# A two-block transformer on one core: small tables moved between the large tiles of SBUF

## The reference, cut to what matters

```python
# first block, layer l: 1024 x 2816 in, 1024 x 1024 out
hx = rmsnorm(x, g_pre) * (1 + scale) + shift
q, k, v, ga, uf, gf, zc, bc, cc, gc = split_cols(hx @ w_in, PROJ_SIZES)
x = x + gate * rmsnorm(gated_merge(a, ga, f, gf, s, gc, w_out), g_post)

# second block, layer l: two gated products around a mixer
x = x + 0.5 * m2 * swiglu(ada_norm(x, g0, m0, m1), ffn_w_in[l, 0], ffn_w_out[l, 0])
x = x + m5 * mixer(ada_norm(x, g1, m3, m4), ...)        # even: attention + mLSTM, odd: GLA
x = x + 0.5 * m8 * swiglu(ada_norm(x, g2, m6, m7), ffn_w_in[l, 1], ffn_w_out[l, 1])

def swiglu(h, w_in, w_out):
    a, b = jnp.split(h @ w_in, 2, axis=-1)              # 1024 -> 2 x 2816
    return (jax.nn.silu(a) * b) @ w_out                 # 2816 -> 1024
```

## Time and profile before

| | |
|---|---|
| runs | 2320.84, 2322.02, 2312.03 us, median 2320.84 |
| span of the profiled execution | 2314.2 us (6.6 us under the median; its own time outside the profiler isn't given) |
| instructions | 46991, of them 19320 matmuls and 19320 weight loads |
| busy | matmul 96%, weight load 90%, VectorE 49%, ScalarE 37%, GpSimd 8% |
| TensorE's granted clock | 0.987 of 2.4 GHz over the span |
| DMA | 312.5 MB read, 135 GB/s over the span |

### The profile page before, as it was taken

One profiled execution on the slowest core, in us unless ns is written; L12 is line 12 of the kernel. 1 busy time (PEld: TensorE's weight loads), 2 busy tenths in 40 slices (PEclk: granted clock), 3 DMA queues, 4 the chain that ended last, 5 costly groups with the idle time before them and its releaser, 6 DMA issues. The chain is left out here.

```text
span 2314.2 us, 46991 instructions
## 1 busy us (share of the span) xinstructions
PE 2227.1 (96%) x19320; PEld 2091.2 (90%) x19320; DVE 1145.4 (49%) x1930; ACT 846.8 (37%) x1384; POOL 176.3 (8%) x150
## 2 busy tenths in 40 slices
PE   6999999899999999998999999999999999999998
PEld 5986798799999999976999999999999998979998
DVE  5227375653433445456653333454343446487665
ACT  4226454632221233248432222243232234455444
POOL 0003112100000010501200000010000010001000
PEclk9999999999999999999999999999999999999999
DMA  9853544445676244520354666242233233225573
GB/s 297 234 167 86 172 133 104 128 147 154 186 216 186 86 131 117 149 80 28 102 175 141 190 207 189 84 126 85 81 114 94 86 96 101 74 82 146 168 202 112
DMA packets 515900, 315.76 MB, mean 136 GB/s; under 512 B 16035, under 2 KB 513274, under 8 KB 515622
## 3 DMA queue, kind: packets, MB, share of 16 engines
q1 hardware_dynamic: 515160, 313.45, 46.1%
q10 hardware_dynamic: 590, 0.16, 0.0%
HBM read 312.50 MB, written 1.06 MB: 135 GB/s over the span
## 5 line engine op out<-in xcount | busy, mean ns | idle before, releaser
L1118 PE MATMUL ps<-h_hi,w_hi 128*128 128x256 f32 x3376 | 728.0, 280 | 3.5 <-DVE h_lo L1726 1.7
L1118 PE MATMUL ps<-h_lo,w_hi 128*128 128x256 f32 x3376 | 720.6, 278 | 0.0
L1118 PE MATMUL ps<-h_hi,w_lo 128*128 128x256 f32 x3376 | 720.6, 278 | 0.0
L1118 PEld LDWEIGHTS ps<-h_hi,w_hi 128*128 128x128 f32 x3376 | 537.8, 189 | 22.9 <-issue 21.6
L1118 PEld LDWEIGHTS ps<-h_lo,w_hi 128*128 128x128 f32 x3376 | 539.4, 189 | 0.1
L1118 PEld LDWEIGHTS ps<-h_hi,w_lo 128*128 128x128 f32 x3376 | 537.9, 189 | 0.0
L1960 DVE TENSOR_TENSOR w_lo<-stage,w_hi 128x1024 fp32r<-128x1024 f32 x227 | 285.0, 1258 | 441.5 <-ACT w_hi L1467 440.9
L1467 ACT ACTIVATE w_hi<-stage 128x1024 fp32r<-128x1024 f32 x227 | 236.6, 1055 | 334.4 <-PE ps L1118 200.4
L1960 DVE TENSOR_TENSOR w_lo<-deep,w_hi 128x1024 fp32r<-128x1024 f32 x184 | 226.1, 1234 | 226.9 <-ACT w_hi L1467 225.2
L1467 ACT ACTIVATE w_hi<-deep 128x1024 fp32r<-128x1024 f32 x184 | 191.9, 1055 | 179.7 <-PE ps L1118 141.4
L1118 PE MATMUL ps<-g_hi,w_hi 128*128 128x256 f32 x1100 | 232.9, 280 | 0.2
(11 more groups left out here) (413 smaller groups left out, 2858.0 us busy)
## 6 DMA issues: line engine op xcount, KB each, us to landing
modw<-in_ada_w SPq DMA_DIRECT2D x72, 1024.0 KB, 6.7
stage<-in_ffn_w_in SPq DMA_DIRECT2D x88, 512.0 KB, 3.9
deep<-in_ffn_w_in SPq DMA_DIRECT2D x88, 512.0 KB, 3.9
modw<-in_w_mod SPq DMA_DIRECT2D x18, 1024.0 KB, 6.1
stage<-in_w_in SPq DMA_DIRECT2D x30, 512.0 KB, 5.3
stage<-in_ffn_w_out SPq DMA_DIRECT2D x32, 384.0 KB, 3.5
stage<-in_even_w_in SPq DMA_DIRECT2D x24, 512.0 KB, 4.0
deep<-in_ffn_w_out SPq DMA_DIRECT2D x32, 384.0 KB, 3.4
```

Source lines behind the costliest of these rows:

```text
L1118: last = mm(ps[:, j, v - a:v - a + SEQ], w_part[wp][:, u % RING, c, :], x_part[xp][:, x, v:v + SEQ], start=first and wp == xp and v == a, ...
```

## The change

The order of the tiles in the stretch is another, and the four `modA` become parts of the stretch. `modA` 0 and 1 (256 bytes) go between `big` and `hT`; `svec` and `modA` 2 and 3 (2944 bytes) go between `vtok` and `stage`. No instruction is added, taken away or moved on any engine, and no tile has another size. The stretch is 1024 bytes longer, and the tiles behind it lie where they lay or 1024 bytes on.

```diff
-        sizes = {"resid": KC * NT, "big": 24 * NT, "hT": KC * NT, "mixT": KC * NT, "vtok": TT * D + TT * ML_HEADS, "stage": STAGE * KC * P,
-                 "scr": 2 * RING * KC * P, "modw": 2 * KC * SEG,
-                 "wfbd": 4 * P, "svec": 2 * KC * 34}
+        sizes = {"resid": KC * NT, "big": 24 * NT, "modA0": 2 * KC * 2, "modA1": 2 * KC * 2, "hT": KC * NT, "mixT": KC * NT,
+                 "vtok": TT * D + TT * ML_HEADS, "svec": 2 * KC * 34, "modA2": 6 * KC * 2, "modA3": 6 * KC * 2, "stage": STAGE * KC * P, "scr": 2 * RING * KC * P,
+                 "modw": 2 * KC * SEG, "wfbd": 4 * P}
...
-        modA = [sb(f"modA{i}", [P, 2 if i < 2 else 6, KC, 2]) for i in range(4)]
+        modA = [over(f"modA{i}", f"modA{i}", 0, [P, 2 if i < 2 else 6, KC, 2]) for i in range(4)]
```

## The result

The changed kernel takes 2355.08 us (median of three runs, 2353.00 to 2356.01) against 2320.84 us before: a ratio of 1.015, with a 95% interval of 1.0128 to 1.0173. It is slower by 34 us at the median. The profiled execution has a span of 2353.3 us, 39.1 us over that of before; its own time is 2355.08 us, 1.8 us above its span.

The account below looks back on a forecast made before the run. TensorE's queue was taken as the bound, so only the distance between products counted: `h` +36.6, `token_pair` -2.5, `g` 0, together +34 us on 2320.8 gives 2355 us; range 2345 to 2361, for 8 in 10 2262 to 2366.

Parts of the forecast that it names:

- What bounds the kernel, and that a transfer or a rounding would be covered.: TensorE's queue bounds nearly all stages, matmuls covering 96% of the span; earlier or later transfers or weight roundings cost nothing.
- Other places of the tables, the transposes: cost 0.: Moved small tables cost ScalarE and VectorE nothing visible; transposes and small-vector products, some hundreds, at most about 2 us either way.
- `token_pair` as the one sight of 448.: `token_pair`, the only row at residue 448, ran at 117.4 ns and never fast, so 448 was read as slow alone.
- `h` loses its fast share, +36.6 us.: Products streaming `h`, moved to residue 448: all 8217 fast distances turn slow at 4.45 ns each, +36.6 us.
- No stretch on `h` at 113.3 ns: Sign of being right: the profile after shows no stretch of products on `h` at the fast distance of 113.3 ns.
- `g` at 192, 0 us within -10.0 and +6.3.: Products streaming `g`, moved to residue 192 with no near row: bounds all fast -10.0, all slow +6.3 us; 0 taken.
- The median of the group: Sign for `g`: its prediction was to be read in its group's median duration, 281 ns before the change.
- `token_pair`, -2.5 us.: `token_pair` gets the residue `h` had; taking the fast rhythm as often, 74% of 762 distances, it gains 2.5 us.
- The sum, +34 us.: Terms of `h`, `token_pair` and `g` together on the profiled span, added to the median of the runs: 2355 us.
- the lower bounds from other products: Rival of a rhythm shorter than any now, chance 0.13 together: 111.6 ns gives 2268 us, 109.2 ns gives 2230 us.
- Nothing: Rival, chance 0.20: interruptions alone choose the rhythm, the residue is idle, every stretch draws anew; 2313 to 2329 us.
- worse: Rival, chance 0.06: residue 448 or 192 gives a distance above 117.8 ns; 2366 us and above.

Follow-up runs that it names:

- 448: Kernel before with 384 unused bytes behind the token tiles, residue 448 against both `h` and `g`: 2354.3 us, ratio 1.0143.
- 320: Kernel before with 256 unused bytes behind the token tiles, residue 320 against both `h` and `g`: 2313.35 us, ratio 0.9999.
- 192: Kernel before with 128 unused bytes behind the token tiles, residue 192 against both `h` and `g`: 2353.23 us, ratio 1.0145.
- 0: Kernel before with 448 unused bytes behind the token tiles, residue 0 against both `h` and `g`: 2391.75 us, ratio 1.0339.
- 96: Kernel before with 32 unused bytes behind the token tiles, residue 96 against both `h` and `g`: 2368.52 us, ratio 1.0205.
- 128: Kernel before with 64 unused bytes behind the token tiles, residue 128 against both `h` and `g`: 2373.3 us, ratio 1.0255.
- 256: Kernel before with 192 unused bytes behind the token tiles, residue 256 against both `h` and `g`: 2393.98 us, ratio 1.0337.
- 288: Kernel before with 224 unused bytes behind the token tiles, residue 288 (32 modulo 256): 2372.95 us, ratio 1.0221.

## Why the prediction was right, step by step

- *What bounds the kernel, and that a transfer or a rounding would be covered.* Right: VectorE's and ScalarE's busy time did not change by more than 1.4 us, and TensorE's idle time fell by 4.0 us.
- *Other places of the tables, the transposes: cost 0.* Right, and shown by the kernel with pads in the tables' stead: 2354.8 us.
- *`token_pair` as the one sight of 448.* This step carried the forecast, and it held: other kernels with 448 against one-piece streams are slow for 89 to 94% of the products on `h`. What I held against it, that `token_pair` streams two pieces, played no part: at 64 or 320 it has the fast rhythm in 31 to 75% of its products (five kernels), at 448 or 192 in none (four kernels).
- *`h` loses its fast share, +36.6 us.* Right in kind, 10% too large: 7% stayed fast, and the term measured 33.1 us. The median of its durations is 279 ns, as forecast, and the loops from 518 us on last 24.90 us in place of 24.06, the forecast 0.84 us each. "No stretch on `h` at 113.3 ns" was wrong: there are eight of over 20 products, the longest of 190.
- *`g` at 192, 0 us within -10.0 and +6.3.* It came out at the upper bound, +6.3 us in the changed kernel. With `h` left at 64 the time rose by 3 us, with an interval from 0, and the share of `g` didn't fall. The choice of 0 had no row behind it, and 192 is in fact a slow residue like 448. The median of the group was a poor sign for it: it fell from 281 to 279 ns while the last fast product on `g` went.
- *`token_pair`, -2.5 us.* -1.0 us: 31% fast, not 74%.
- *The sum, +34 us.* The terms measured give +38.3 us on the profiled spans, and the medians moved by +34.2 us. That the forecast met the median to 0.1 us is luck in part: the three terms' errors (-3.5, +6.3, +1.5) leave +4.3 us, and what made them up is that the profiled execution of before was a fast one of its kind, while that of after was the median itself. In all runs the time is 1.8 us above the span, so of the 6.6 us that the prediction added some 4.8 us were that one execution's luck.
- *The rivals.* No run had a rhythm shorter than the fast one of 113.3 ns, so the lower bounds from other products were never met (111.6 ns for those of line 2522 and 109.2 for the transposes of line 2584, means over the trace of before, of which the earlier trace rows has two stretches). "Nothing" fell with the result and with the kernels with 448 and 192 for both. That rival took the 10 us between runs of one program for the draw of the rhythms; part of it is not: at residue 0, which has one rhythm alone, four runs still lie 5.5 us apart, and their granted clocks from 0.988 (2388.49 us) to 0.985 (2394.01 us). What "worse" took for unlikely exists, but at 0, 32, 96 and 128, not at the residues of the change.
- *That the residue is not idle.* With the same instructions in the same order the mean distance goes from 114.6 ns at 320 to 119.9 ns at 0, and the median time from 2313.35 to 2391.75 us. What inside the chip makes the difference no run shows; only that it depends on the distance between the two addresses modulo 256, and, as far as a shift of both by 128 bytes tells (`h` 80% fast at 64, with the weights where they lay for 8% at 192), not on the addresses themselves.

## What to carry to other kernels

Where weight loads and matmuls of 256 columns alternate, look in the trace for pure stretches of one instruction and divide their length by the count: two values at one clock, here 113.3 and 117.8 ns at 1.00, mean that something beside the shapes is at work. The place of the loaded operand against the streamed one, modulo 256 bytes, is then worth a sweep in steps of 32, with unused bytes and nothing else changed; here 64 was the best of the six tried (2313 to 2321 us), and 0, which comes by itself when all tiles are multiples of 256 bytes long, the worst (2391.8 and 2394.0 us), 3.4% slower than before. No layout tried was faster than the kernel before, and 320 was equal to it. An operand that appears in both roles, as in `token_pair`, shows another residue for free before any run is made: it stood at 117.4 ns at 448 in the kernel before, and `h` then at 117.7 ns at 448.

## What the runs showed of the hardware that was not expected

Times and mean distances of the large products by residue, where it is the same for `h` and `g` (a product is a weight load of 128 columns and a stream of 256). The last two columns take in `token_pair`, 5% of the products, which stands at the negative of the residue. "Fast" is every distance under 116 ns; at 32, 96 and 128 these are nearly all 115 ns, single values in a changing sequence and not the rhythm of 113.3 ns:

| residue modulo 256 | kernels | time us | mean distance ns | fast share, all |
|---|---|---|---|---|
| 0 | 0, 256 | 2391.8, 2394.0 | 119.9 | 0% |
| 32 | 288 | 2373.0 | 118.3 | 4% |
| 64 | before (64), all moved by 256 (64), 320 | 2320.8, 2317.3, 2313.4 | 115.1, 115.0, 114.6 | 62%, 64%, 73% |
| 96 | 96 | 2368.5 | 118.1 | 12% |
| 128 | 128 | 2373.3 | 118.8 | 17% |
| 192 | 192, 448 | 2353.2, 2354.3 | 117.4 | 10%, 8% |

The kernel before was run again beside each set and stood at 2314 to 2320 us. Three things were not expected: that 0 is a stable rhythm of its own at 119.9 ns, slower than any that the kernel before showed; that 32 bytes to either side of 64 cost 48 and 53 us; and that a single distance, of 220 to 223 or of 224 to 228 ns, at the start of a stretch tells in 386 of 422 entries which rhythm follows. Residues 160 and 224 were not tried for `h` and `g`; `token_pair` alone stood there, at 120.0 and 117.2 ns.
